# A retention head's output made token by token, normed by ScalarE sums along the row, and turned afterwards

## The chip, the cores and the metric

One NeuronCore of one Trainium2 chip runs the whole program. The metric is device time in microseconds (us) of one execution. The engines are TensorE (PE; its weight loads are shown apart as PEld), VectorE (DVE), ScalarE (ACT), GpSimd (POOL) and SyncE (SP), which issues the weight stream's transfers. They run their own instruction lists and meet only at semaphores.

## The reference, cut to what matters

The program is one block with sparse attention (8 heads of 64) and retention (4 heads, keys 128 wide, values 256 wide) on 512 tokens by 1024 features, a feed-forward part, and then two layers of another block. The change lies in the retention heads:

```
def head_group_norm(o, w):
    mean = jnp.mean(o, axis=-1, keepdims=True)
    var = jnp.mean(jnp.square(o - mean), axis=-1, keepdims=True)
    return (o - mean) * lax.rsqrt(var + EPS) * w.astype(jnp.float32)
...
o = o_inner + jnp.moveaxis(o_cross, 0, 1)
...
o_r = head_group_norm(o_r, ret_gn_w[layer]) * jax.nn.silu(g_ret...)
y_b = o_r.astype(x.dtype).reshape(B, S, RET_V_W) @ w_ret_branch[layer]
```

For each head `o` is (masked, decayed scores) times values: 512 tokens by 256 features. Each token is normed over its 256 features and multiplied by the gate silu(g).

## The kernel before, in words

**Layout.** Activations lie with features on the 128 partitions and the 512 tokens along the row. The weights stream in as units of 128x1024; PE makes one output tile of a unit from 24 matmuls of 128x512 (for each of 8 slices k: `w_hi*a_hi`, `w_hi*a_lo`, `w_lo*a_hi`, L832 to L834), since each operand is split into a rounded high part and the rest. ACT makes `w_hi` (`hi_part`, L434), POOL makes `w_lo` (`lo_part`, L377, four instructions a unit), DVE takes the result out of its bank (L1392).

**The retention stage.** It has 4 heads t = 0 to 3 of 8 slots j = 0 to 7. A slot is one unit on PE, with other work laid between its slices k by `beside`. Beside each retention head runs one attention query head: in slot j PE makes scores (L1028), DVE their maxima (L1586 to L1592), ACT the exponentials with row sums (L548), DVE the probabilities (L1618 to L1624), PE turns these with transposes (L1035, L1036; placed at k = 6, or k = 5 in slots 3 and 7), ACT copies the turned tiles out of the banks (`copy_transposed`, L557, into `pt`), and PE multiplies them by the values (L1047). The order on every engine is written out by hand, so a waiting instruction holds all that stands behind it. After the unit of a slot PE waits for the copied probabilities (`probs_copied`), then makes the scores of the next slot (not in slot 7) and the value products. The next head's first scores follow those of slot 7.

**The head's output before.** In slot 6 (`retention_products(5)`) `ret_values` makes the output with features on partitions: values stationary, decayed scores `rp` moving, for both halves e of the features, into banks `b_r0` and `b_r1` (L1015). ACT copies both out (L613, L614) into `rq` and `rk` (tiles of `h`). DVE adds the two, PE multiplies the sum by a matrix of ones (L1077, slot 7, k = 3), DVE takes the mean off (L1832), squares and adds (L1836 to L1839) into `ssum`, PE sums these with ones (`square_sum`, L867, behind the unit of slot 7), and ACT takes the root (`tile_root`, L458), for which it loads a table and then the exponentials' table again. In the next head DVE inverts the root in four pieces (`inverse_root`, L1733), and POOL multiplies gate by output (`gate_output`, L395) and by the inverse (`scale_output`, L403) between its `lo_part` instructions. ACT and DVE then split the result into `y_hi` (`output_hi`, L570) and `y_lo` (`output_lo`, L1746).

**ACT in slot 7**: the exponentials, `hi_part`, two copies that turn the next query's halves (`turn_query`, L527), a table load and the gate's Silu (L623, tile `rg`), the copy of the turned probabilities (L557), table, root, table.

**The end of the stage**: PE starts the next part, U_YA, whose first two units it does in two pieces (slices k = 0 to 2 of both, then k = 3 of both, which wait for `attention_out_rounded`). Unit 2 of U_YA needs the banks of unit 0, which DVE empties with two multiplications (L1865). DVE copies one element (L1856) to signal `tables_used`, on which ACT's transfer of x into `h` waits.

Of the kernel before, what the change touches and what calls it, by code (L numbers as in the profile page):

```python
# [147 lines left out]
def build(nc, stream, xT, tab, decay, rope, par1, par2, pT, out):  # L148
    ctx = ExitStack()
    with ctx:  # L150
# [68 lines left out]
        head_sum = token_root  # L219
        hid = w1(at + 256, 128).rearrange("p (k c) -> p k c", c=64)  # L220
# [5 lines left out]
        rq, rk = h[:, 4, :], h[:, 5, :]  # L226
        qt, q_turned = tile_d, m[:, 7, :]
# [68 lines left out]
        root_inverted = sem("root_inverted")  # L296
        output_gated = sem("output_gated")
        output_scaled = sem("output_scaled")
# [70 lines left out]
        def _(pool):  # L369
# [17 lines left out]
            def quarters():  # L387
                return [(e, slice(c * S // 2, (c + 1) * S // 2)) for e in range(2) for c in range(2)]

            def gate_output(t):  # L390

                pool.wait_ge(activated, t + 2)
                pool.wait_ge(squares_ready, t + 2)
                for e, cols in quarters():
                    pool.tensor_tensor(rg[:, e, cols], rg[:, e, cols], (rq, rk)[e][:, cols], ALU.mult)\  # L395
                        .then_inc(output_gated, 1)

            def scale_output(t):

                pool.wait_ge(output_gated, 4 * t + 4)  # L400
                pool.wait_ge(root_inverted, t + 1)
                for e, cols in quarters():
                    pool.tensor_tensor(rg[:, e, cols], rg[:, e, cols], ssum[:, cols], ALU.mult)\  # L403
                        .then_inc(output_scaled, 1)
# [18 lines left out]
        def _(act):  # L423
# [142 lines left out]
            def output_hi(t):  # L566

                act.wait_ge(output_scaled, 4 * t + 4)
# [52 lines left out]

# [192 lines left out]
        def _(pe):  # L814
# [181 lines left out]
            for t in range(RH):  # L996
# [14 lines left out]
                def ret_values(e, dst):  # L1011
                    at = 0
                    for a in range(QT):
                        n = S - a * P
                        ins = pe.matmul(dst[:, a * P:S], rv[:, a, e * P:(e + 1) * P], rp[:, at:at + n],  # L1015
                                        start=a == 0, stop=a == QT - 1, skip_group_check=True)
                        at += n
                    ins.then_inc(product_ready, rps.up())
# [32 lines left out]
                def retention_products(j):  # L1051
# [17 lines left out]
                    if j == 5:  # L1069
                        pe.wait_ge(product_read, rfree.due())  # L1070
                        pe.wait_ge(value_rows_copied, 2 * t + 2)
                        ret_values(0, b_r0)
                        ret_values(1, b_r1)
# [1457 lines left out]
```

## Time and profile before

| | |
|---|---|
| time, 3 runs | 2577.57 us median (2577.47 to 2578.15) |
| the profiled execution | 2577.84 us, span 2576.1 us |
| PE busy | 2558.5 us of the span (99%) |
| DVE, ACT, POOL busy | 1486.3, 838.6, 1514.9 us |
| granted TensorE clock over the span | 1.00 |

A matmul's shown duration includes its way through the array, so neighbouring matmuls overlap in the rows; what one costs is the distance from its start to the next one's start. A multiplication of two unrounded fp32 operands is shown as two matmul records, a transpose as one. "Idle before" in brackets is the time an engine stood idle, and behind the arrow what ended it.

### The profile page before, as it was taken

The page shows a single profiled execution, that of the slowest core. Times are in us where ns is not written, and L with a number is a line of the kernel's source. Part 1 is how long each engine was busy: PE and PEld are TensorE (multiplying, and loading weights), DVE is VectorE, ACT ScalarE, POOL GpSimd, SP SyncE. Part 2 cuts the span into 40 slices and gives each one's busy share as a digit, 9 for nine tenths or more (in the row PEclk, how much of TensorE's full clock was granted, in tenths as well). Part 3 has the DMA queues.
Part 4 walks back from the last instruction along what each step waited for, and adds up shares of the span by engine and source line. Part 5 has one row for each costly group of instructions (what it writes and reads, how often), then busy time and mean ns, then how long its engine had stood idle before and what let it go on. Part 6 is the DMA issues. An engine that isn't in the chain of part 4 may idle for free.

```text
span 2576.1 us, 32876 instructions
## 1 busy us (share of the span) xinstructions
PE 2558.5 (99%) x11723; PEld 2062.5 (80%) x11723; DVE 1486.3 (58%) x2084; ACT 838.6 (33%) x1157; POOL 1514.9 (59%) x1820
## 2 busy tenths in 40 slices
PE   8999999999999999999999999999999999999999
PEld 7767778888888887778888888888778888888887
DVE  7756774487474737845583442754773448344275
ACT  5444442233222343354321111134334432111112
POOL 7634446666666755555565655765554556565576
PEclk9999999999999999999999999999999999999999
DMA  5311113222222332222322222233222222222223
GB/s 208 115 66 50 55 61 131 98 83 98 99 97 98 109 111 82 83 82 82 106 99 98 98 97 92 89 114 105 77 85 84 82 106 98 99 98 97 92 89 130
DMA packets 36829, 247.44 MB, mean 96 GB/s; under 512 B 4464, under 2 KB 4848, under 8 KB 7792
## 3 DMA queue, kind: packets, MB, share of 16 engines
q1 hardware_dynamic: 34704, 238.57, 26.2%
q10 hardware_dynamic: 2016, 7.35, 0.8%
q8 instruction: 76, 1.25, 0.2%
q14 instruction: 33, 0.27, 0.0%
HBM read 243.81 MB, written 2.10 MB: 95 GB/s over the span
## 4 chain that ended last, share of the span: by engine, by line
PE 31%; POOL 30%; issue 22%; DVE 0%; POOLq 0%; DMA 0%; ACT 0%; DVEq 0%; SPq 0%; ACTq 0%
POOL w_lo L377 30%; PE bank L832 7%; PE bank L834 7%; PE bank L833 7%; PE both L833 3%; PE both L834 3%; PE both L832 3%; PE bank L1281 0%; PE both L1257 0%; PE bank L1243 0%; PE bank L1241 0%; PE bank L1242 0%; DMA raw<-stream 0%; POOLq L415 0%; POOLq L374 0%
## 5 line engine op out<-in xcount | busy, mean ns | idle before, releaser
L377 POOL TENSOR_TENSOR w_lo<-raw,w_hi 128x256 fp32r<-128x256 f32 x1784 | 1492.6, 868 | 964.2 <-ACT w_hi L434 963.2
L434 ACT ACTIVATE w_hi<-raw 128x1024 fp32r<-128x1024 f32 x446 | 469.1, 1056 | 981.6 <-PE bank L834 476.8
L832 PE MATMUL bank<-a_hi,w_hi 128*128 128x512 f32 x1440 | 582.1, 404 | 0.0
L834 PE MATMUL bank<-a_hi,w_lo 128*128 128x512 f32 x1440 | 562.3, 390 | 0.0
L833 PE MATMUL bank<-a_lo,w_hi 128*128 128x512 f32 x1440 | 561.3, 390 | 0.0
L832 PEld LDWEIGHTS bank<-a_hi,w_hi 128*128 128x128 f32 x1440 | 270.5, 188 | 63.7 <-issue 10.3
L834 PEld LDWEIGHTS bank<-a_hi,w_lo 128*128 128x128 f32 x1440 | 270.3, 188 | 58.3
L833 PEld LDWEIGHTS bank<-a_lo,w_hi 128*128 128x128 f32 x1440 | 270.9, 188 | 54.7 <-issue 3.1
L832 PE MATMUL bank<-y_hi,w_hi 128*128 128x512 f32 x696 | 272.4, 391 | 0.0
L834 PE MATMUL bank<-y_hi,w_lo 128*128 128x512 f32 x696 | 270.9, 389 | 0.0
L833 PE MATMUL bank<-y_lo,w_hi 128*128 128x512 f32 x696 | 270.8, 389 | 0.0
L832 PE MATMUL both<-a_hi,w_hi 128*128 128x512 f32 x560 | 219.1, 391 | 0.0
L834 PE MATMUL both<-a_hi,w_lo 128*128 128x512 f32 x560 | 217.9, 389 | 0.0
L833 PE MATMUL both<-a_lo,w_hi 128*128 128x512 f32 x560 | 217.9, 389 | 0.0
L832 PE MATMUL both<-y_hi,w_hi 128*128 128x512 f32 x504 | 196.5, 390 | 0.5 <-DVE y_lo L1398 0.2
L834 PE MATMUL both<-y_hi,w_lo 128*128 128x512 f32 x504 | 196.1, 389 | 0.0
L833 PE MATMUL both<-y_lo,w_hi 128*128 128x512 f32 x504 | 196.1, 389 | 0.0
L832 PEld LDWEIGHTS bank<-y_hi,w_hi 128*128 128x128 f32 x696 | 130.7, 188 | 27.3 <-issue 0.5
L834 PEld LDWEIGHTS bank<-y_hi,w_lo 128*128 128x128 f32 x696 | 130.6, 188 | 27.3
L833 PEld LDWEIGHTS bank<-y_lo,w_hi 128*128 128x128 f32 x696 | 130.7, 188 | 27.2 <-issue 0.5
L548 ACT ACTIVATE prob<-both,small 128x128 f32<-128x128 f32 (+3 forms) x128 | 66.3, 523 | 203.0 <-DVE small L1592 202.8
L1890 DVE TENSOR_TENSOR h<-bank,h 128x512 f32<-128x512 f32 x56 | 38.7, 691 | 154.5 <-PE bank L834 153.8
(343 smaller groups left out, 3279.6 us busy)
## 6 DMA issues: line engine op xcount, KB each, us to landing
raw<-stream SPq DMA_DIRECT2D x223, 1024.0 KB, 4.8
h<-xT SPq DMA_DIRECT2D x8, 256.0 KB, 5.9
h<-xT ACTq DMA_DIRECT2D x1, 2048.0 KB, 8.1
outT<-h SPq DMA_DIRECT2D x8, 256.0 KB, 2.3
h<-decay ACTq DMA_DIRECT2D x1, 1024.0 KB, 4.8
h<-rope ACTq DMA_DIRECT2D x1, 1024.0 KB, 9.3
prob<-pT ACTq DMA_DIRECT2D x2, 512.0 KB, 4.4
par<-par ACTq DMA_DIRECT2D x2, 408.0 KB, 3.3
```

The costliest lines, as they stand in the source:

```text
L377: pool.tensor_tensor(w_lo[:, s, part], raw[:, s, part], w_hi[:, s, part], ALU.subtract).then_inc(lo_done, 1)
L434: act.activation(w_hi[:, s, cols], raw[:, s, cols], ACT.Copy).then_inc(hi_done, 1)
L548: ins = act.activation(dst, src, ACT.Exp, bias=small[:, b:b + 1], scale=last_scale, accum_out=small[:, b + 4:b + 5])
L832: pe.matmul(dst, w_hi[:, s, cols], rhs_hi(k), start=start and k == 0, stop=False)
L833: pe.matmul(dst, w_hi[:, s, cols], rhs_lo(k), start=False, stop=False)
L834: ins = pe.matmul(dst, w_lo[:, s, cols], rhs_hi(k), start=False, stop=stop and k == nk - 1)
L1890: leave(u0, j, V.tensor_tensor(h[:, n, :], bank4(j), h[:, n, :], ALU.add))
```

## The change

- `ret_values(i)` now makes the output with tokens on partitions: for token tile i (four of 128) the pieces of `rp` are stationary and the values, 256 columns, move: 10 matmuls instead of 8, the same number of columns in all. Tiles 0 and 1 lie in `b_r0`, 2 and 3 in `b_r1`.
- ACT copies the four tiles of 128x256 out with a row sum each (`accum_out`), where it made two copies of 128x512.
- In slot 7 DVE scales the four sums to means (`output_mean`); ACT, ahead of the gate's Silu, squares the four tiles with the mean as bias, again with a row sum; it takes the root of a 128x4 tile instead of a 128x512 one.
- Both multiplications by ones on PE (L1077 and the `square_sum` of the stage) are gone, and DVE's sum, mean, squares and the four-piece inversion.
- In slot 0 of the next head DVE inverts 128x4 numbers and scales the four tiles by mean and root (`output_norm`). In slot 1, k = 3, PE turns the tiles with eight transposes back into `b_r0`, `b_r1` (`turn_outputs`), and DVE multiplies them by the gate (`output_gate`).
- POOL does none of this any more.
- For the last head `turn_outputs` stands on PE between the two pieces of U_YA's units 0, 1 and unit 2, and `output_gate` on DVE ahead of the `tables_used` copy and of U_YA's multiplications.

```diff
@@ gpsimd
-                    if j == 7 and t > 0:
-                        scale_output(t - 1)
-                    if j == 10:
-                        gate_output(t)
                     lo_part(t * RET_UNITS + U_RET + j, j % 4)
-            scale_output(RH - 1)
@@ scalar, slots 6 and 7
                     if j == 6:
                         rps.up(2)
                         act.wait_ge(product_ready, rps.now())
-                        act.activation(rq, b_r0[:, :], ACT.Copy).then_inc(outputs_copied, 1)
-                        act.activation(rk, b_r1[:, :], ACT.Copy).then_inc(outputs_copied, 1)
-                        rps.up(1)
+                        for i, rows in enumerate(out_rows):
+                            ins = act.activation(rows, (b_r0, b_r1)[i // 2][:, i % 2 * RDV:(i % 2 + 1) * RDV],
+                                                 ACT.Copy, accum_out=out_mean[:, i:i + 1])
+                        ins.then_inc(outputs_copied, 1)
                     if j == 7:
-
+                        act.wait_ge(output_mean_ready, t + 1)
+                        for i, rows in enumerate(out_rows):
+                            ins = act.activation((ssum[:, :], tile_c)[i // 2][:, i % 2 * RDV:(i % 2 + 1) * RDV], rows, ACT.Square,
+                                                 bias=out_mean[:, i:i + 1], accum_out=out_root[:, i:i + 1])
+                        ins.then_inc(output_squares_done, 1)
                         act.wait_ge(evac, u0 + 11)
                         act.activation(rg, rg, ACT.Silu).then_inc(activated, res.up())
                     copy_transposed([(pt[:, :, 0:n], scores[:, :, 0:n])])
                     if j == 7:
-                        tile_root(ssum[:, :], b_r1[:, :], 1.0 / RDV)
+                        load_table(ACT.Sqrt)
+                        act.wait_ge(output_squares_done, t + 1)
+                        act.activation(out_root, out_root, ACT.Sqrt, bias=eps, scale=1.0 / RDV)\
+                            .then_inc(root_ready, root.up())
                         load_table(ACT.Exp if t < RH - 1 else ACT.Sigmoid)
@@ tensor
+                def ret_values(i):
+                    dst = (b_r0, b_r1)[i // 2][:, i % 2 * RDV:(i % 2 + 1) * RDV]
+                    for a in range(i + 1):
+                        at = sum(S - c * P for c in range(a)) + (i - a) * P
+                        ins = pe.matmul(dst, rp[:, at:at + P], rv[:, a, :], start=a == 0, stop=a == i,
+                                        skip_group_check=True)
+                    if i % 2 == 1:
+                        ins.then_inc(product_ready, rps.up())
+
+                def turn_outputs(t):
+
+                    pe.wait_ge(output_normed, t + 1)
+                    for e in range(2):
+                        for i in range(QT):
+                            ins = pe.transpose((b_r0, b_r1)[e][:, i * P:(i + 1) * P],
+                                               out_rows[i][:, e * P:(e + 1) * P], ident)
+                    ins.then_inc(output_turned, 1)
@@
-                    if j == 6:
-                        pe.wait_ge(outputs_copied, 2 * t + 2)
-                        pe.wait_ge(retention_input_ready, rin.due())
-                        pe.matmul(b_r0[:, :], ones, tile_c, start=True, stop=True)\
-                            .then_inc(product_ready, rps.up())
@@
+                    if k == 3 and j == 1 and t > 0:
+                        turn_outputs(t - 1)
@@
-                    if j == 7:
-                        square_sum()
@@ behind the two pieces of U_YA's units 0 and 1
+            turn_outputs(RH - 1)
@@ vector
+            def output_norm(t):
+
+                V.wait_ge(root_ready, root.due())
+                V.reciprocal(out_root, out_root).then_inc(vector_step, steps.up())
+                V.wait_ge(vector_step, steps.now())
+                for i, rows in enumerate(out_rows):
+                    ins = V.tensor_scalar(rows, rows, out_mean[:, i:i + 1], out_root[:, i:i + 1],
+                                          ALU.add, ALU.mult)
+                ins.then_inc(output_normed, 1)
+
+            def output_gate(t):
+
+                V.wait_ge(activated, res.due())
+                V.wait_ge(output_turned, t + 1)
+                for e in range(2):
+                    V.tensor_tensor(rg[:, e, :], (b_r0, b_r1)[e][:, :], rg[:, e, :], ALU.mult)\
+                        .then_inc(output_gated, 1)
@@
                 if last is not None and j == 0:
                     attention_out(last, 1)
+                    output_norm(last)
+                if last is not None and j == 1:
+                    output_gate(last)
@@ behind the stage
             attention_out(RH - 1, 1)
+            output_norm(RH - 1)
             attention_rounded(RH - 1, 1)
-            for quarter in range(4):
-                inverse_root(RH - 1, quarter)
-            V.wait_ge(output_gated, 4 * RH)
+            output_gate(RH - 1)
+            V.wait_ge(output_gated, 2 * RH)
             V.tensor_copy(small[:, 20:21], rq[:, 0:1]).then_inc(tables_used, 1)
```

Where the instructions stand is shown at three places, first before and then changed. The first is ACT's list in slot 7 of a head (the second one), from `hi_part` to the first table load behind the copy of the turned probabilities.

```order
L434 ACTIVATE w_hi<-raw 128x1024 [waits unit_done,block_landed_1]
L527 ACTIVATE m<-m 64x512 x2
L623 ACT_TABLE_LOAD
L623 ACTIVATE rg<-rg 128x1024 [waits unit_evacuated]
L557 ACTIVATE pt<-both 128x1024 [waits probs_transposed,values_added]
L450 ACT_TABLE_LOAD
```

```order
L415 ACTIVATE w_hi<-raw 128x1024 [waits unit_done,block_landed_1]
L508 ACTIVATE m<-m 64x512 x2
L605 ACTIVATE ssum,small<-h,small 128x256 [waits output_mean_ready]
L605 ACTIVATE ssum,small<-h,small 128x256
L605 ACTIVATE tile_c,small<-h,small 128x256 x2
L609 ACT_TABLE_LOAD
L609 ACTIVATE rg<-rg 128x1024 [waits unit_evacuated]
L538 ACTIVATE pt<-both 128x1024 [waits probs_transposed,values_added]
L431 ACT_TABLE_LOAD
```

Four squares (L605), the first of which waits for `output_mean_ready`, now stand between `turn_query` (L508) and the table load of the Silu, and so ahead of the copy into `pt` (L538, before L557). The second place is DVE's list from the last probabilities of slot 0 of the second head through slot 1 up to the maxima of slot 2.

```order
L1709 TENSOR_TENSOR cmp_prob<-bank,ta 64x512 [waits lower_half_copied,probs_ready]
L1586 TENSOR_TENSOR both<-both,cst 128x2x128 [waits scores_ready,attention_out_read]
L1589 TENSOR_REDUCE small<-both 128x2 [waits vector_step]
L1592 TENSOR_SCALAR small<-small 128x2 [waits vector_step]
L1392 TENSOR_TENSOR ta<-bank,rstd 128x512 [waits unit_done,vector_step,max_ready]
L1439 STREAM_SHUFFLE tb<-ta 128x512 [waits unit_evacuated]
L1618 RECIPROCAL small<-small 128x2 [waits exp_ready]
L1621 TENSOR_SCALAR prob<-prob,small 128x256 [waits vector_step]
L1624 TENSOR_SCALAR prob<-prob,small 128x256 [waits vector_step]
L1447 TENSOR_TENSOR tb<-tb,h 128x512 [waits vector_step,probs_ready]
L1448 TENSOR_TENSOR ta<-ta,h 128x512
L1586 TENSOR_TENSOR both<-both,cst 128x2x128 [waits scores_ready]
```

```order
L1703 TENSOR_TENSOR cmp_prob<-bank,ta 64x512 [waits lower_half_copied,probs_ready]
L1725 RECIPROCAL small<-small 128x4 [waits root_ready,attention_out_read]
L1728 TENSOR_SCALAR h<-h,small 128x256 [waits vector_step]
L1728 TENSOR_SCALAR h<-h,small 128x256 x3
L1580 TENSOR_TENSOR both<-both,cst 128x2x128 [waits scores_ready]
...
L1615 TENSOR_SCALAR prob<-prob,small 128x256 [waits vector_step]
L1618 TENSOR_SCALAR prob<-prob,small 128x256 [waits vector_step]
L1737 TENSOR_TENSOR rg<-bank,rg 128x512 [waits output_turned,activated,probs_ready]
L1737 TENSOR_TENSOR rg<-bank,rg 128x512
L1441 TENSOR_TENSOR tb<-tb,h 128x512 [waits vector_step]
L1442 TENSOR_TENSOR ta<-ta,h 128x512
L1580 TENSOR_TENSOR both<-both,cst 128x2x128 [waits scores_ready]
```

The inversion and four scalings (L1725, L1728) came in between `attention_out` (L1703) and the maxima of slot 1 (L1580), and two multiplications (L1737) between the probabilities of slot 1 and the two products L1441, L1442. The third place is the end of the stage on DVE, from `attention_out` of the last head to the multiplications that empty the banks of U_YA's unit 0.

```order
L1709 TENSOR_TENSOR cmp_prob<-bank,ta 64x512 [waits lower_half_copied]
L1718 TENSOR_TENSOR cmp_prob<-cmp_prob,vn 64x512 [waits cmp_out_copied,attention_out_read]
L1722 CAST y_hi<-cmp_prob 64x512 [waits vector_step]
L1724 TENSOR_TENSOR y_lo<-cmp_prob,y_hi 64x512 [waits vector_step]
L1733 RECIPROCAL ssum<-ssum 128x128 [waits root_ready,attention_out_rounded]
L1733 RECIPROCAL ssum<-ssum 128x128 x3
L1856 COPY small<-h 128x1 [waits output_gated,root_inverted,vector_step]
L1865 TENSOR_TENSOR m<-both,m 128x512 [waits vector_step,unit_done,activated,to_activate]
L1865 TENSOR_TENSOR m<-both,m 128x512
```

```order
L1703 TENSOR_TENSOR cmp_prob<-bank,ta 64x512 [waits lower_half_copied]
L1725 RECIPROCAL small<-small 128x4 [waits root_ready,attention_out_read]
L1728 TENSOR_SCALAR h<-h,small 128x256 [waits vector_step]
L1728 TENSOR_SCALAR h<-h,small 128x256 x3
L1712 TENSOR_TENSOR cmp_prob<-cmp_prob,vn 64x512 [waits cmp_out_copied]
L1716 CAST y_hi<-cmp_prob 64x512 [waits vector_step]
L1718 TENSOR_TENSOR y_lo<-cmp_prob,y_hi 64x512 [waits vector_step]
L1737 TENSOR_TENSOR rg<-bank,rg 128x512 [waits output_turned,activated,attention_out_rounded]
L1737 TENSOR_TENSOR rg<-bank,rg 128x512
L1842 COPY small<-h 128x1 [waits output_gated]
L1851 TENSOR_TENSOR m<-both,m 128x512 [waits vector_step,unit_done,activated,to_activate]
L1851 TENSOR_TENSOR m<-both,m 128x512
```

The first of the two L1737 waits for `output_turned`, which PE gives behind both pieces of U_YA's units 0 and 1, and all that stands behind it, L1851 (before L1865) included, comes after it.

## Rows read from the trace of the kernel before

**Rows 1.** The page: busy time by engine, share of the span, instructions.

```profile
PE 2558.5 (99%) x11723; PEld 2062.5 (80%) x11723; DVE 1486.3 (58%) x2084; ACT 838.6 (33%) x1157; POOL 1514.9 (59%) x1820
```

**Rows 2.** Timeline of PE, third head, slots 6 and 7.

```profile
291.74 4.47 PE L1015 MATMUL bank<-work 128*128 128x512 f32 x16
...
306.57 0.27 PE L1035 MATMUL both<-cst,prob 128*128 128x128 f32 x1
...
307.34 0.27 PE L1036 MATMUL both<-cst,prob 128*128 128x128 f32 x1
...
309.30 0.40 PE L834 MATMUL bank<-a_hi,w_lo 128*128 128x512 f32 x1
309.85 1.13 PE L867 MATMUL bank<-ssum,cst 128*128 128x512 f32 x2 [0.15 <-DVE ssum L1839]
310.90 1.09 PE L1047 MATMUL bank<-pt,work 128*64 128x128 f32 x16
```

**Rows 3.** Timeline of PE's weight loads, slot 7, first head.

```profile
164.72 0.85 PEld L1047 LDWEIGHTS bank<-pt,work 128*64 128x64 f32 x16 [0.81 <-ACT pt L557]
```

**Rows 4.** Timeline of ACT, third head, slots 6 and 7; last row first head.

```profile
299.07 0.81 ACT L557 ACTIVATE pt<-both 128x768 f32<-128x768 f32 x1 [0.51 <-PE both L1036]
...
305.89 1.28 ACT L527 ACTIVATE m<-m 64x512 f32<-64x512 f32 x2
307.19 1.28 ACT L623 ACT_TABLE_LOAD   x1
308.48 1.06 ACT L623 ACTIVATE rg<-rg 128x1024 f32<-128x1024 f32 x1
309.45 1.00 ACT L557 ACTIVATE pt<-both 128x1024 f32<-128x1024 f32 x1
...
163.66 1.00 ACT L557 ACTIVATE pt<-both 128x1024 f32<-128x1024 f32 x1
```

**Rows 5.** Timeline of ACT, two exponentials of 256 columns with a row sum.

```profile
320.49 0.47 ACT L548 ACTIVATE prob<-both,small 128x256 f32<-128x256 f32 x1 [3.05 <-DVE small L1592]
...
320.95 0.47 ACT L548 ACTIVATE prob<-both,small 128x256 f32<-128x256 f32 x1
```

**Rows 6.** Timelines, slot 7: DVE third head, DVE fourth head, PE fourth head.

```profile
305.80 0.55 DVE L1624 TENSOR_SCALAR prob<-prob,small 128x512 f32<-128x512 f32 x1
...
377.01 0.55 DVE L1624 TENSOR_SCALAR prob<-prob,small 128x512 f32<-128x512 f32 x1
...
382.12 1.09 PE L1047 MATMUL bank<-pt,work 128*64 128x128 f32 x16
```

**Rows 7.** Timeline of DVE, third head, slots 1 and 2; last row POOL.

```profile
247.88 0.43 DVE L1586 TENSOR_TENSOR both<-both,cst 128x256 f32<-128x256 f32 x1 [2.37 <-PE both L1028]
...
250.96 0.41 DVE L1621 TENSOR_SCALAR prob<-prob,small 128x256 f32<-128x256 f32 x1
251.41 0.80 DVE L1624 TENSOR_SCALAR prob<-prob,small 128x256 f32<-128x256 f32 x1
...
255.21 0.43 DVE L1586 TENSOR_TENSOR both<-both,cst 128x256 f32<-128x256 f32 x1 [0.71 <-PE both L1028]
...
251.32 3.76 POOL L377 TENSOR_TENSOR w_lo<-raw,w_hi 128x256 fp32r<-128x256 f32 x4 [3.11 <-ACT w_hi L434]
```

**Rows 8.** Timelines of DVE, then PE, at U_YA's unit 2.

```profile
393.12 1.29 DVE L1865 TENSOR_TENSOR m<-both,m 128x512 f32<-128x512 f32 x2 [1.24 <-PE both L834]
...
394.55 0.47 PE L832 MATMUL both<-y_hi,w_hi 128*128 128x512 f32 x1 [0.21 <-DVE m L1865]
```

**Rows 9.** Timeline of PE at the program's start.

```profile
8.17 0.77 PE L902 MATMUL both<-a_hi,w_hi 128*128 128x512 f32 x1 [8.17 <-DVE a_lo L1473]
...
11.30 0.63 PE L903 MATMUL both<-a_lo,w_hi 128*128 128x512 f32 x1
11.72 0.62 PE L902 MATMUL both<-a_hi,w_hi 128*128 128x512 f32 x1
...
12.41 0.39 PE L902 MATMUL both<-a_hi,w_hi 128*128 128x512 f32 x1
```

More of the change, by code:

```diff
@@ L219, in build @@
         head_sum = token_root
+        out_mean = small[:, 16:20]
+        out_root = small[:, 0:16].rearrange("p (i c) -> p i c", c=4)[:, :, 2]
         hid = w1(at + 256, 128).rearrange("p (k c) -> p k c", c=64)
@@ L226, in build @@
         rq, rk = h[:, 4, :], h[:, 5, :]
+        out_rows = [(rq, rk)[i // 2][:, i % 2 * RDV:(i % 2 + 1) * RDV] for i in range(QT)]
         qt, q_turned = tile_d, m[:, 7, :]
@@ L295, in build @@
         gelu_ready = sem("gelu_ready")
-        root_inverted = sem("root_inverted")
         output_gated = sem("output_gated")
-        output_scaled = sem("output_scaled")
+        output_mean_ready = sem("output_mean_ready")
+        output_squares_done = sem("output_squares_done")
+        output_normed = sem("output_normed")
+        output_turned = sem("output_turned")
         output_rounded = sem("output_rounded")
@@ L1009, in ret_transposes @@
                     ins.then_inc(product_ready, rps.up())
[L1011 to L1018, printed above, removed]
+                def ret_values(i):
[13 more added lines that the diff above has]
+                    ins.then_inc(output_turned, 1)
                 def attention_scores(j):
@@ L1071, in retention_products @@
                         pe.wait_ge(value_rows_copied, 2 * t + 2)
-                        ret_values(0, b_r0)
-                        ret_values(1, b_r1)
-                    if j == 6:
-                        pe.wait_ge(outputs_copied, 2 * t + 2)
-                        pe.wait_ge(retention_input_ready, rin.due())
-                        pe.matmul(b_r0[:, :], ones, tile_c, start=True, stop=True)\
-                            .then_inc(product_ready, rps.up())
+                        for i in range(QT):
+                            ret_values(i)
                 def compressed_branch(j):
@@ L1726, in attention_rounded @@
                 V.wait_ge(attention_out_rounded, rounded.now())
-            def inverse_root(t, quarter):
-                if quarter == 0:
-                    V.wait_ge(root_ready, root.due())
-                cols = slice(quarter * P, (quarter + 1) * P)
-                ins = V.reciprocal(ssum[:, cols], ssum[:, cols])
-                if quarter < 3:
-                    ins.then_inc(vector_step, steps.up())
-                else:
-                    V.wait_ge(vector_step, steps.now())
-                    ins.then_inc(root_inverted, 1)
-                    V.wait_ge(root_inverted, t + 1)
-                    res.due()
+            def output_norm(t):
[12 more added lines that the diff above has]
+                        .then_inc(output_gated, 1)
             def output_lo(t):
@@ L1749, in output_lo, with output_mean @@
                 V.wait_ge(y_tile_ready, y_rdy.now())
-            def outputs_in(t):
-                V.wait_ge(outputs_copied, 2 * t + 2)
+            def output_mean(t):
+                V.wait_ge(outputs_copied, t + 1)
                 rps.due(2)
-                V.tensor_tensor(tile_c, rq, rk, ALU.add).then_inc(retention_input_ready, rin.up())
-                V.wait_ge(retention_input_ready, rin.now())
+                V.tensor_scalar(out_mean, out_mean, -1.0 / RDV, None, ALU.mult).then_inc(output_mean_ready, 1)
             def slot(t, j):
@@ L1764, in slot @@
                     if last is not None:
-                        V.wait_ge(output_gated, 4 * last + 4)
+                        V.wait_ge(output_gated, 2 * last + 2)
                     rope_sum(rq).then_inc(vector_step, steps.up())
@@ L1811, in slot @@
                     compressed_product()
-                if last is not None and j in (3, 4):
-                    inverse_root(last, 2 * j - 6)
-                    inverse_root(last, 2 * j - 5)
                 if j == 5:
@@ L1827, in slot @@
                 if j == 7:
-                    V.wait_ge(product_ready, rps.due())
+                    output_mean(t)
                     V.tensor_copy(small[:, 24:26], par[:, C1_GN + 2 * t:C1_GN + 2 * t + 2])\
                         .then_inc(vector_step, steps.up())
-                    for o in (rq, rk):
-                        V.scalar_tensor_tensor(out=o, in0=b_r0[:, :], scalar=-1.0 / RDV, in1=o,
-                                               op0=ALU.mult, op1=ALU.add)\
-                            .then_inc(vector_step, steps.up())
                     V.wait_ge(vector_step, steps.now())
-                    V.tensor_tensor(tile_a, rq, rq, ALU.mult).then_inc(vector_step, steps.up())
-                    V.tensor_tensor(ssum[:, :], rk, rk, ALU.mult).then_inc(vector_step, steps.up())
-                    V.wait_ge(vector_step, steps.now())
-                    V.tensor_tensor(ssum[:, :], ssum[:, :], tile_a, ALU.add)\
-                        .then_inc(squares_ready, sums.up())
-                    V.wait_ge(squares_ready, sums.now())
                     if t < RH - 1:
```

17 lines of the change are left out of this document (1 added, 16 removed).

## The prediction, made before the changed kernel was run

> **What bounds the kernel now.** I read the page first: PE is busy for 99% of the span, every other engine for 59% or less [rows 1]. So a change counts only by what it takes from PE's instruction list, puts into it, or makes PE wait for. Then the timeline of PE through the stage. In slot 7 of the third head the unit's last matmul starts at 309.30, the multiplication by ones (`square_sum`, L867) at 309.85 after 0.15 us of idle, and the value products (L1047) at 310.90 [rows 2]. The reader is to see that PE hardly waits, and that L867 fills the time in which ACT still works on what L1047 reads: ACT's copy into `pt` begins at 309.45 and lasts 1.00, to 310.45, which is 0.45 before L1047 starts [rows 4]. In the first head there is no such room: the copy ends at 163.66 + 1.00 = 164.66, and L1047's weight load starts at 164.72, released by it [rows 3, 4]. DVE is as close: it finishes the probabilities at 305.80 + 0.55 = 306.35, and the transposes that read them start at 306.57, their weight load before them [rows 2, 6]. So slot 7 is where PE, ACT and DVE meet, and the change works on all three there.
>
> **PE's own work.** `ret_values` moves the same columns: 8 matmuls with 2,560 columns before, 10 of 256 after. Before, the 16 records run 4.4 us [rows 2]; between records of 128 and of 512 columns no pause shows in that sum, so I take 0 for it, 0.4 as the upper end for all heads together. Eight transposes come in: from 306.57 to 307.34 there are seven steps of 0.11, so eight cost 0.88 us a head, 3.5 us for four. The `square_sum` goes: 310.90 less 309.85 is 1.05, and with the idle before it up to 1.3. L1077, a matmul of the same shape, goes too, about 0.9. If nothing waited, PE would gain 4 x (1.3 + 0.9) and lose 3.5.
>
> **What takes the place of L1077.** It stands at k = 3 of slot 7, ahead of the transposes. Without it PE is at the transposes 0.9 earlier, but the probabilities are ready at 306.35 as before, since DVE's and ACT's work for them starts from the scores of slot 6. PE was there about when they were; now it waits. Worth: nothing.
>
> **What takes the place of `square_sum`.** ACT gets four squares between `turn_query` and the Silu's table load, ahead of the `pt` copy. No row before has a square with bias and row sum; the nearest is the exponential of 256 columns with both, a start every 320.95 - 320.49 = 0.46 us [rows 5]. It reads from a bank, the square from SBUF. The upper end is the 64x512 copy from SBUF, 1.28 for two, 0.64 each [rows 4]; the lower 0.40. I take 0.46, the same form, and 0.15 for the last sum's own end: 2.0 us. The Trainium skill (ScalarE: Activation LUTs, What ACT_TABLE_LOAD costs) gives 280 ns + 0.833 ns a column for an instruction with a pointer as bias, less 93 ns of overlap; by that page it would be 0.40 each without the sum's reading, 1.6 in all.
> Behind the squares stand the table load (1.28), the Silu (0.97 from start to start) and the copy (1.00), all unchanged [rows 4]. In the third head: squares start at 307.19, when DVE's mean is there (306.35 + about 0.2). The copy ends at 310.45 + 2.0 = 312.45, L1047 starts at 312.5 in place of 310.90: +1.6. The second head's slot 7 has the same order, +1.6. In the first head L1047 already hung on the copy: +2.0. In the fourth there is no `turn_query`, so ACT waits for the mean: 377.01 + 0.55 + 0.2 [rows 6]. POOL is no longer held at `gate_output` then, so its `lo_part` starts beside DVE's last probabilities and can stretch them as in [rows 7]: I add 0.4. That is 378.2, + 2.0 + 1.28 + 0.97 + 1.0 = 383.4, against L1047 at 382.12 [rows 6]: +1.3. Sum of the four: 6.5 us. PE thus stands about 2.9 us idle behind the unit of slot 7 (309.53 to 312.5), where it stood 0.15. ACT's table, root, table follow the copy as before; the root of 128x4 is shorter, so the next head's first exponentials move with PE and cost nothing more.
>
> **Slot 6.** The four copies with sums are at most 4 x 0.46 in place of 2 x 0.5, so up to 0.85 later for ACT; it stood idle 0.51 ahead of its next copy into `pt` [rows 4]. Cost 0, upper end 0.3 a head in three heads.
>
> **DVE in the next head's slots 0 and 1.** The four scalings of 256 columns come ahead of the maxima of slot 1, the two gate multiplications (0.65 each, as L1865 with a bank as source [rows 8]) ahead of slot 2's. DVE's idle there is 2.37 and 0.71 [rows 7], and PE comes 0.88 later in slot 1: 3.96 in all. A scaling of 256 columns took 0.41 alone and 0.80 beside POOL [rows 7]. Alone: 4 x 0.45 + 0.2 + 1.35 = 3.35, no stall. Beside POOL: 4 x 0.84 + 0.2 + 1.35 = 4.9, about 1 us late. POOL's `lo_part` runs in slot 0 at just that place, and DVE has little idle time until slot 3, so I take 0.5 us a head for three heads, 1.5 us; ends 0 and 1.2 a head. The Trainium skill (SBUF — State Buffer, Who interferes with whom) holds that a VectorE scaling in its two-port mode and a GpSimd instruction exclude each other for a whole instruction; by that rule each scaling could wait a whole POOL instruction, and this term would go to its upper end. The 0.80 against 0.41 agrees.
> DVE no longer does the sum, squares and inversion (3.4 us behind the last head); no row shows PE waiting for them but the 0.15 above, so that is worth nothing more.
>
> **The end of the stage.** `turn_outputs` of the last head stands behind both pieces of U_YA's units 0 and 1, and DVE's `output_gate` waits for it ahead of the multiplications that empty unit 0's banks. Before, DVE did these from 393.12 while PE worked on unit 1, and PE's unit 2 waited 0.21 [rows 8]. Now, from the end of the transposes: 1.3 for the two gate multiplications, 0.2 for the one-element copy, 1.29 for L1865, and about 0.2 of hand-over: PE is idle 3.0, so +2.8. Queued behind on ACT: the transfer of x, which waits for `tables_used`, and two weight units; they are needed slots later.
>
> **The sum**, against the profiled execution of 2577.84 us: slot 7 +6.5, transposes +3.5, lateness of DVE +1.5, end of the stage +2.8, together +14.3: 2592.1. The median is 0.27 below that execution, so 2591.8 us.
>
> **Rivals.**
> *PE's lighter list decides (faster).* If ACT's copy were done when PE has finished its unit, PE would gain 4 x 2.2 - 3.5 = 5.3: 2572.3. For it the copy must end at 309.6 in the third head; it ends at 310.45 without any square, so even free squares leave L1047 no earlier than 310.5. Against it as well: the probabilities at 306.35. Chance 0.04.
> *It cancels (within 0.2%).* With squares that cost hardly anything, no lateness of DVE: slot 7 comes to -1, transposes 3.5, end 2.8: +5, about 2582.8. The exponentials' 0.46 speaks against it. Chance 0.07.
> *The clock falls.* PE now stands idle some 3 us four or five times. At the start, after 8.17 us of idle, its 512-column matmuls began 0.42 apart and showed 0.63, later 0.39 [rows 9]: the lower of 1.2 and 2.4 GHz, though the granted clock reads 1.00. If each wait brings some 4 us at that rate, each costs 2 us more: +8 to +10, 2601. No row shows an idle stretch of 3 us inside the program, so none excludes it. The Trainium skill (TensorE: Matmul & The Clock Gate, Part 1) says that idleness throttles the clock back, and that busy time releases it. The start agrees. Chance 0.10.
> *DVE is the new bound in slots 0 to 3.* If the gate multiplications are stretched too, each of three heads is 2 us late at slot 3: 2591.8 + 4.5 = 2596.3. Chance 0.14.
> *The forecast*: 0.65, with its own range 2587 to 2596.
>
> **How the numbers follow.** A measurement of this kernel can tell about 0.2%, 5.2 us, from no change. Low end: squares 0.40 (-1.0), no lateness (-1.5), no stretching (-0.4), end of stage 0.5 less: +10.9, 2588; I go to 2586.5, half-way to the case that cancels. High end: squares 0.64 (+2.9), lateness 1.2 a head (+2.1), slot 6 (+0.9), `ret_values` (+0.4): 2598.1; with a part of the clock's case 2599.5. Faster 0.04, same 0.07, slower 0.89.
>
> **What would show it.** L1047 of slot 7 released by ACT's copy, with PE idle about 2.9 us before it in three heads; the transposes of slot 7 released by DVE's probabilities after 0.8 of idle; squares 0.46 apart; about 3 us idle ahead of U_YA's unit 2, released by DVE's L1851; PE's busy time down by some 5 us while the span grows. It would be wrong if the squares take under 0.2 each, if ACT's idle time hides them, or if DVE's maxima of slots 1 to 3 slip by more than 1 us.

## The result and the profile after

| | before | after |
|---|---|---|
| time, median | 2577.86 us (2577.47 to 2578.66, 4 runs) | 2599.39 us (2599.12 to 2600.13, 4 runs) |
| ratio | | 1.0084, 95% interval 1.0072 to 1.0097 |
| span of the profiled execution | 2576.1 us | 2597.3 us |
| granted TensorE clock, mean | 1.000 | 0.996 |

The change costs 21.5 us. The page of the changed kernel gives for the engines:

```profile
PE 2563.6 (99%) x11755; PEld 2074.9 (80%) x11755; DVE 1471.4 (57%) x2076; ACT 847.3 (33%) x1213; POOL 1495.5 (58%) x1788
```

PE's busy time rose by 5.1 us against [rows 1], though the added transposes (3.5 us) are less than the multiplications by ones that went (some 7 us). So something made the same matmuls longer. The view of what PE waited for (engine, line, what it waited for: us in total, times, longest) names the new waits:

```profile
PE bank L1045 <- ACT pt L538: 12.4, 4, 3.5
...
PE both L821 <- DVE m L1851: 3.1, 1, 3.1
PE both L1033 <- DVE prob L1618: 2.7, 5, 0.7
```

Of the five waits for L1618 two, in the first head's early slots, stood before too (0.61 and 0.69 then, 0.32 and 0.69 now); three of 0.55 are new. Slot 7 of the second head, on ACT and then on PE (timelines; the value products, L1047 before, are L1045 now, the transposes L1033, the query scores L1026):

```profile
239.12 1.28 ACT L508 ACTIVATE m<-m 64x512 f32<-64x512 f32 x2
240.42 0.51 ACT L605 ACTIVATE ssum<-h,small 128x256 f32<-128x256 f32 x1
...
241.92 0.49 ACT L605 ACTIVATE tile_c<-h,small 128x256 f32<-128x256 f32 x1
...
242.52 1.28 ACT L609 ACT_TABLE_LOAD   x1
243.81 1.06 ACT L609 ACTIVATE rg<-rg 128x1024 f32<-128x1024 f32 x1
244.78 1.00 ACT L538 ACTIVATE pt<-both 128x1024 f32<-128x1024 f32 x1
```

```profile
239.63 0.33 PE L1033 MATMUL both<-cst,prob 128*128 128x128 f32 x1 [0.55 <-DVE prob L1618]
...
242.41 0.40 PE L823 MATMUL bank<-a_hi,w_lo 128*128 128x512 f32 x1
245.83 1.14 PE L1045 MATMUL bank<-pt,work 128*64 128x128 f32 x16 [3.02 <-ACT pt L538]
246.90 0.58 PE L1026 MATMUL both<-work,td 64*128 64x128 f32 x1
...
248.65 0.63 PE L823 MATMUL bank<-a_hi,w_lo 128*128 128x512 f32 x1
249.08 0.63 PE L821 MATMUL bank<-a_hi,w_hi 128*128 128x512 f32 x1
```

The four squares take from 240.42 to 242.52, and table load, Silu and copy follow without a gap; the copy ends at 245.78 and PE, idle since 242.81, starts at 245.83. This is the third head's picture of [rows 2, 4] with the copy 2.1 us later. Ahead of it PE waits 0.55 for DVE's probabilities, in the place of L1077. New is what stands behind the wait: the unit's matmuls start 0.43 us apart and show 0.63, as at the program's start [rows 9]. Granted clock by stretch of the changed kernel (columns: stretch, length, busy time and count of PE, PEld, DVE, ACT, POOL, granted clock, DMA share, GB/s), each from the end of a long wait, and one stretch behind slot 3 of the second head for comparison:

```profile
166.70:174.00 7.30, 7.27 (x39) 5.82 (x40) 4.84 (x12) 5.40 (x11) 1.76 (x3) 0.77 0.01 2
205.70:213.00 7.30, 7.30 (x49) 6.03 (x48) 6.72 (x13) 3.33 (x8) 3.56 (x4) 1.00 0.00 0
245.80:254.00 8.20, 8.17 (x44) 6.53 (x45) 5.68 (x13) 5.85 (x12) 2.59 (x4) 0.79 0.01 2
321.10:329.00 7.90, 7.90 (x43) 6.27 (x44) 5.25 (x12) 5.73 (x12) 2.16 (x3) 0.78 0.01 2
396.10:404.00 7.90, 7.86 (x39) 6.30 (x40) 3.87 (x9) 7.83 (x9) 0.00 (x0) 0.78 0.01 2
413.80:421.00 7.20, 7.13 (x24) 5.76 (x25) 1.24 (x2) 0.07 (x1) 2.80 (x4) 0.76 0.90 349
```

All five stretches behind waits of 2.8 to 3.5 us have 0.76 to 0.79, which is part of the time at 1.2 GHz and part at 2.4; the other has 1.00.

The last head's output, on PE and DVE, with the rows that answer to [rows 8]:

```profile
409.76 1.03 PE L1014 MATMUL bank<-cst,h 128*128 128x128 f32 x8
413.87 0.64 PE L821 MATMUL both<-y_hi,w_hi 128*128 128x512 f32 x1 [3.07 <-DVE m L1851]
414.31 0.63 PE L822 MATMUL both<-y_lo,w_hi 128*128 128x512 f32 x1
...
410.93 1.29 DVE L1737 TENSOR_TENSOR rg<-bank,rg 128x512 f32<-128x512 f32 x2 [6.75 <-PE bank L1014]
412.25 0.15 DVE L1842 COPY small<-h 128x1 f32<-128x1 f32 x1
412.43 1.29 DVE L1851 TENSOR_TENSOR m<-both,m 128x512 f32<-128x512 f32 x2
```

The eight transposes (L1014) run first, then DVE's two gate multiplications (L1737, L1842 is the one-element copy), then what empties the banks (L1851); PE stands idle 3.07 where it stood 0.21, and goes on at half rate.

**Where the 21 us are.** From one head's value products of slot 7 to the next one's the rows give 74.97, 71.21 and 71.22 us before and 79.10, 75.27 and 75.04 after. The first head's are 2.01 later, the way from the fourth's to U_YA's unit 2 is 17.73 in place of 12.43, and the 24 matmuls of that unit take 7.14 in place of 5.56. Together 2.01 + 4.13 + 4.06 + 3.82 + 5.30 + 1.58 = 20.9 of the span's 21.2. What of it is the clock follows from the starts of the same instructions before and after, from the value products to where the matmuls are 0.23 apart again: 1.55, 1.50, 1.51 and 1.55 us longer than before, and 1.58 in the last unit. A head's eight transposes take 0.79 to the next matmul's start, and that matmul's own step is 0.08 longer, 0.87 together; the last head's cost 0.88. What is left of each way between heads is slot 7's. So:

| | forecast | measured |
|---|---|---|
| slot 7, four heads | 6.5 | 2.0 + 1.7 + 1.7 + 1.4 = 6.8 |
| transposes | 3.5 | 3 x 0.87 + 0.88 = 3.5 |
| DVE late in slots 0 to 3 | 1.5 | 0 |
| end of the stage | 2.8 | 3.07 - 0.21 = 2.9 |
| half-rate matmuls | 0 | 7.7 |
| sum | 14.3 | 20.9 |

### The profile page after: what moved, and what is told of

It is laid out like the page before. It is cut to its first block, busy times and chain, and to the rows that moved or that the text cites. A ratio compares the mean times of both kernels' runs of the same rounds, so it can differ in the third digit from the quotient of the medians.

```text
span 2597.3 us, 32939 instructions
## 1 busy us (share of the span) xinstructions
PE 2563.6 (99%) x11755; PEld 2074.9 (80%) x11755; DVE 1471.4 (57%) x2076; ACT 847.3 (33%) x1213; POOL 1495.5 (58%) x1788
## 4 chain that ended last, share of the span: by engine, by line
PE 40%; POOL 32%; issue 23%; ACT 2%; DVE 1%; DMA 1%; POOLq 0%; SPq 0%; DVEq 0%; ACTq 0%
POOL w_lo L382 32%; PE bank L821 9%; PE bank L823 8%; PE bank L822 8%; PE both L821 3%; PE both L823 3%; PE both L822 3%; DMA raw<-stream 1%; PE both L1026 1%; PE bank L1004 1%; PE bank L1045 1%; PE bank L1275 0%; PE both L1251 0%; ACT w_hi L415 0%; PE bank L1237 0%
```

## The experiments

All ratios are to the kernel before, measured beside each experiment on the same chip (2577.80 and 2577.74 us there, 2577.86 above, so that a difference to the changed kernel carries about 0.1 us of doubt from this). Three theories were to be told apart: that PE's idle stretches cost time twice, as waits and by the clock behind them (A); that the slow matmuls come from something else in the new order, and idleness is not their cause (B); and that the late engine is not ACT's squares but something that only moves when they are moved (C).

**Squares in slot 6.** The mean goes to DVE's slot 6 and the squares behind slot 6's copy on ACT, where ACT stood idle 3.6 us; the lines taken out stood in slot 7, ahead of the Silu.

```diff
-                        act.wait_ge(output_mean_ready, t + 1)
-                        for i, rows in enumerate(out_rows):
-                            ins = act.activation(..., rows, ACT.Square, ...)
...
                     copy_transposed([(pt[:, :, 0:n], scores[:, :, 0:n])])
+                    if j == 6:
+                        act.wait_ge(output_mean_ready, t + 1)
+                        for i, rows in enumerate(out_rows):
+                            ins = act.activation(..., rows, ACT.Square, ...)
...
@@ vector
                 if j == 6:
+                    output_mean(t)
...
                 if j == 7:
-                    output_mean(t)
```

> The changed kernel with the mean on DVE and the four squares on ACT moved from slot 7 to slot 6, behind that slot's copy of the turned probabilities. Theory A (ACT's squares make PE wait about 3 us in slot 7 of each head, and the wait lets TensorE's clock fall, so that the next matmuls run at half rate): the waits shrink from 3.0 to 3.5 us to about 1 to 1.5, the matmuls behind them stay about 0.23 us apart, and the time falls by 4 x 2.1 + 6.3 = 14.7 us, to about 2585. Theory B (the slow matmuls behind the wait come from something else in the new order, not from the idle time): only the squares' time comes back, 8.4 us, 2591, and the slow matmuls stay. Theory C (moving the squares makes slot 6 or slot 7's exponentials late instead): less than 8 us.

Measured: 2583.47 us (2581.41 to 2584.7), ratio 1.0021 (1.0011 to 1.0030), 15.9 us less than the changed kernel. PE's waits for ACT's copy and for U_YA's banks, and the granted clock behind the first and second head's slot 7 and behind U_YA's wait:

```profile
PE bank L1046 <- ACT pt L538: 3.3, 3, 1.4
PE both L822 <- DVE m L1852: 3.1, 1, 3.1
```

```profile
164.80:172.00 7.20, 7.17 (x46) 5.75 (x46) 4.75 (x12) 5.78 (x12) 1.66 (x3) 1.00 0.01 2
240.20:248.00 7.80, 7.74 (x50) 6.05 (x50) 5.31 (x12) 5.80 (x13) 2.22 (x4) 1.00 0.01 2
...
398.70:406.00 7.30, 7.25 (x25) 5.88 (x26) 1.23 (x2) 0.06 (x1) 2.80 (x4) 0.78 0.91 352
```

Waits of 1.4 and 0.9 us are left, the clock behind them is 1.00, and only U_YA's wait of 3.07 is still followed by 0.78. This is A's case, and C is out. Since the edit also moves work, it does not by itself exclude B; the run that fills the wait does.

**The end of the stage redone**, in the changed kernel. `silu_done` is the Silu's count, taken where `output_gate` stood.

```diff
-            turn_outputs(RH - 1)
             for j in range(2, YA_UNITS):
                 unit(U_YA, j, 2, [bank4(2 * j), bank4(2 * j + 1)], y_op(8), 4)
+                if j == 2:
+                    turn_outputs(RH - 1)
@@ vector
-            output_gate(RH - 1)
-            V.wait_ge(output_gated, 2 * RH)
-            V.tensor_copy(small[:, 20:21], rq[:, 0:1]).then_inc(tables_used, 1)
...
                 leave(U_YA, j, ins)
+                if j == 2:
+                    output_gate(RH - 1, silu_done)
+                    V.wait_ge(output_gated, 2 * RH)
+                    V.tensor_copy(small[:, 20:21], rq[:, 0:1]).then_inc(tables_used, 1)
```

> The changed kernel with only the end of the stage redone: the last head's eight transposes stand behind U_YA's unit 2 on PE, DVE's gate multiplications and the tables_used copy behind the emptying of unit 2's banks. Theory A: the idle 3.07 us ahead of unit 2 goes and with it 1.7 us of half-rate matmuls behind it, so about 4.7 us less, 2594.7. Theory B (slow matmuls not from idle time): 3 us less, 2596.4. Theory C: the gate's wait only moves to a later unit, and nothing is gained.

Measured: 2595.35 us (2595.06 to 2595.53), ratio 1.0067 (1.0050 to 1.0083): 4.0 us less than the changed kernel, against 4.7 expected by A and 3 by B. PE's wait there, from the same view as above:

```profile
PE both L821 <- DVE m L1850: 0.2, 1, 0.2
```

The four waits of slot 7 are all there still. The time alone lies between A and B, but the trace decides: the granted clock behind the second head's slot 7 and in U_YA's unit 2 (stretches as above):

```profile
245.70:253.70 8.00, 7.94 (x36) 6.34 (x37) 4.62 (x11) 5.52 (x12) 1.54 (x3) 0.60 0.01 2
411.50:419.00 7.50, 7.43 (x37) 6.26 (x38) 2.81 (x5) 0.00 (x0) 2.56 (x4) 1.00 0.21 87
```

With the wait gone U_YA runs at the full rate, as A has it: 2.9 of waiting and 1.6 of half rate are saved. In this execution the lower level lasted longer behind the second head's wait of 3.02, 2.9 us lost in place of 1.5, and what follows unit 2 took 0.5 less: 2.9 + 1.6 - 1.4 + 0.5 = 3.6, the difference of the two spans (2597.3 and 2593.7).

**PE's wait filled with work.** The sharpest test of A: the changed kernel, with three multiplications into a bank that nobody reads behind the unit of slot 7.

```diff
+                    if j == 7:
+                        pe.wait_ge(outputs_copied, t + 1)
+                        for _ in range(3):
+                            pe.matmul(b_r0[:, :], ones, cst[:, 0:S], start=True, stop=True)
                     pe.wait_ge(probs_copied, ptr.due())
```

> The changed kernel with work added to PE: behind the unit of slot 7 of each head, three multiplications of 128x512 constants by ones into a bank that nobody reads (2.6 us of PE work a head), where PE otherwise stands idle. Theory A: the added work lies in the wait, the clock stays at its upper level, the next matmuls are 0.23 us apart, and the kernel gets faster by about 6.3 us although it does more: 2593. Theory B (the cause is not PE's idleness): no change or up to 1 us slower, and the matmuls behind L1045 stay 0.43 apart.

Measured: 2592.14 us (2590.82 to 2593.33), ratio 1.0054 (1.0038 to 1.0071): 7.3 us faster than the changed kernel, with 12 multiplications of 0.86 (10 us) more work on PE. PE's wait for ACT's copy, and the granted clock behind the second head's slot 7 and behind U_YA's wait, which was left as it is:

```profile
PE bank L1045 <- ACT pt L538: 2.1, 4, 0.9
```

```profile
244.00:252.00 8.00, 7.96 (x50) 6.05 (x50) 5.53 (x13) 5.79 (x12) 2.44 (x4) 1.00 0.01 2
...
407.40:415.00 7.60, 7.52 (x26) 6.11 (x27) 1.35 (x3) 0.22 (x2) 2.83 (x4) 0.78 0.90 349
```

Nothing else was touched: the value products still start when ACT's copy ends, and ACT's list is the same. The ways from one head's value products to the next one's and on to U_YA are 1.58, 1.52, 1.51 and 1.57 us shorter, which are the half-rate terms of the table within 0.03; 0.6 of the rest lies in what follows U_YA's unit 2, and is not explained. So it is PE's standing idle, and not the order of the work, that makes the matmuls behind it slow. B is out.

**ACT's weight alone, on the kernel before.** Four squares of constants ahead of the Silu of slot 7; both multiplications by ones stay.

```diff
                     if j == 7:
+                        for i in range(4):
+                            act.activation(y_lo[:, 6 + i // 2, i % 2 * 256:(i % 2 + 1) * 256], cst[:, 0:256],
+                                           ACT.Square, bias=eps, accum_out=small[:, 16 + i:17 + i])
                         act.wait_ge(evac, u0 + 11)
```

> The kernel before, with nothing of the change but its weight on ACT: four squares of 128x256 constants with a row sum ahead of the gate's Silu in slot 7, into a tile that is free. It still has both multiplications by ones. Theory A: ACT's copy ends 2.0 us later, L1047 starts 1.6 us later in three heads and 2.0 in the first, 6.8 us in all, 2584.6; PE's idle time ahead of it is only about 1.7 us, since square_sum still stands there, and no half-rate matmuls follow. If a wait of 1.7 us is enough for the clock to fall: about 13 us, 2591. If the squares don't hold up PE: no change.

Measured: 2584.97 us (2584.34 to 2587.21), ratio 1.0030 (1.0019 to 1.0040), +7.2. PE's value products of slot 7 in the first two heads, and the clock behind them:

```profile
166.44 1.09 PE L1049 MATMUL bank<-pt,work 128*64 128x128 f32 x16 [2.08 <-ACT pt L557]
...
244.66 1.09 PE L1049 MATMUL bank<-pt,work 128*64 128x128 f32 x16 [1.63 <-ACT pt L557]
```

```profile
166.40:174.00 7.60, 7.56 (x41) 6.06 (x42) 3.82 (x8) 5.79 (x11) 6.34 (x10) 0.78 0.01 2
244.60:252.00 7.40, 7.34 (x46) 5.75 (x46) 3.85 (x8) 6.19 (x13) 6.19 (x10) 1.00 0.01 2
```

Two things came out. The squares alone hold PE up by 1.7 us in three heads; in the fourth, where no `turn_query` stands ahead of them, by little (idle 0.17), since these squares wait for no mean. And an idle stretch of 2.08 brought the clock down, one of 1.63 did not. The value products of the first head start 1.7 later than before, the way from them to the second head's is 3.25 longer, to the third head's 1.7, to the fourth's 0.2. With 1.55 of half rate inside the 3.25 that is 1.7 + 1.7 + 1.7 + 0.2 of waiting, 6.9 of the 7.2 in all, but not as I had split it: I had expected no fall at all, and the fourth head's 1.6. The eight times fall in two groups, five of 2584.3 to 2585.2 us and three of 2587.0 to 2587.2. The profile is of one of the five; whether one more fall makes the others is not shown.

**A third of the filling.** As above, with one multiplication instead of three. One execution only.

> The changed kernel with one multiplication of constants by ones (0.86 us of PE work) instead of three behind the unit of slot 7. PE's idle time there should be 2.6 us in the first head and about 2.1, 2.1 and 1.9 in the others. In the earlier runs idle stretches of 2.8 us and more, and one of 2.08, were followed by matmuls at half rate, stretches of 1.63 and less were not. Theory A: the first head's is followed by half-rate matmuls, the others are near the bound and can go either way; time between 2593 and 2599. Theory B (idleness is not the cause): half-rate matmuls as in the changed kernel in all four.

Measured: 2599.45 us, as slow as the changed kernel. Granted clock behind the waits of 2.65, 2.16, 2.16 and 1.96 us (first to fourth head) and of 3.07 (U_YA):

```profile
166.40:174.00 7.60, 7.60 (x41) 6.03 (x42) 4.79 (x12) 5.48 (x11) 1.71 (x3) 0.78 0.01 2
245.40:253.00 7.60, 7.54 (x41) 6.15 (x42) 4.22 (x11) 5.53 (x12) 1.13 (x2) 0.78 0.01 2
320.70:329.00 8.30, 8.25 (x36) 6.55 (x37) 4.92 (x12) 5.51 (x11) 1.84 (x3) 0.60 0.01 2
397.30:405.00 7.70, 7.65 (x45) 6.36 (x46) 3.66 (x9) 7.62 (x9) 0.00 (x0) 1.00 0.00 0
413.50:421.00 7.50, 7.50 (x21) 5.95 (x22) 1.18 (x2) 0.01 (x1) 2.80 (x4) 0.60 0.91 342
```

The shortest wait is followed by no fall, the other four are, two of them with 0.60 in place of 0.78: there the lower level lasted longer (3.1 and 2.9 us lost in place of 1.5 and 1.6), which made up for the head that was spared. Here a third of the filling was worth nothing, the whole of it 7.3 us.

**Both moved.** Squares in slot 6 and the end of the stage redone (the edits of the first two experiments together).

> The changed kernel with both edits of the first runs: mean and squares in slot 6, and the last head's transposes and gate behind U_YA's unit 2. Theory A adds them up: 2583.5 less 3.1 of idle and 1.6 of half-rate matmuls at the end of the stage, 2578.8, which this measurement cannot tell from the kernel before. No half-rate matmuls inside the program at all. If the two overlap: 2580 to 2583.

Measured: 2578.82 us (2578.52 to 2579.43), ratio 1.0004 (0.9995 to 1.0013). No wait above 1.41 us is left inside the program, and no half-rate matmul in the stage either. So the two edits give back 20.6 of the 21.5 us; the tokens-first output as such costs nothing that this measurement can tell, and gains nothing.

**The copy ahead of the Silu**, on top of that, to take away the waits of 0.9 to 1.4 us that are left in slot 7.

```diff
+                        copy_transposed([(pt[:, :, 0:n], scores[:, :, 0:n])])
                         act.wait_ge(evac, u0 + 11)
                         act.activation(rg, rg, ACT.Silu).then_inc(activated, res.up())
-                    copy_transposed([(pt[:, :, 0:n], scores[:, :, 0:n])])
+                    if j < 7:
+                        copy_transposed([(pt[:, :, 0:n], scores[:, :, 0:n])])
```

> e5 with ACT's copy of the turned probabilities in slot 7 ahead of the Silu and its table load. Theory A: PE's idle time of 0.92 to 1.41 us ahead of the value products goes (3.5 us over four heads). But ACT still has three table loads behind it before the next head's exponentials, about 6.1 us with Silu and root, so these come about 1.4 us later than PE's scores allow, against a room of about 0.5 before the transposes of slot 0: up to 0.9 us of new idle time in three heads. Together 1 to 3.5 us less than e5: 2575.3 to 2578. Rival: the Silu's tables don't matter, and all 3.5 us come back.

Measured: 2578.58 us (2578.34 to 2579.35), ratio 1.0003 (0.9994 to 1.0012): nothing gained, a miss. The waits for ACT's copy are gone from slot 7, but PE waits anew for the probabilities of slot 0 of the third head (timeline), and in total (waits):

```profile
244.75 0.33 PE L1036 MATMUL both<-cst,prob 128*128 128x128 f32 x1 [0.66 <-DVE prob L1622]
```

```profile
PE both L1036 <- DVE prob L1622: 4.7, 8, 0.7
```

Of the eight, two are the old ones of the first head, three are slot 7's 0.55 and three are new, in slot 0. ACT's three table loads between the copy and the next head's exponentials decide there: the last ends at 242.76 and the exponentials start at 242.88, while PE was 1.6 us earlier at the value products than without the edit (238.28 against 239.84). The mechanism was the expected one, up to 0.9 us in each of three heads, and it took 0.75 + 0.66 + 0.67 = 2.1. Against it stand the 1.41 + 0.92 + 0.92 = 3.2 of the waits taken away. That leaves 1.1, of which the time shows 0.2. The starts of the same instructions in both traces say where the rest went. The first head keeps 0.5 of what its slot 7 gives. In the third head PE is 0.59 ahead of the run before up to slot 7, 1.59 ahead at the value products, 0.71 behind slot 0's transposes and 0.58 behind slot 1's, so that two slots take back the whole 1.0. In the fourth head 0.44 of the 0.59 is lost in U_YA, at the matmul that waits for DVE's `attention_rounded` in the next run.

**And the transposes of slot 7 one slice later** (`k == (5 if j == 3 else 6)`).

> e6 with the transposes of slot 7 at k = 6 instead of k = 5, so that PE has 0.7 us more work before it needs DVE's probabilities, for which it now idles 0.56. If only slot 7 decided, 4 x 0.56 = 2.2 us less than e6. If ACT's chain of table loads to the next head's first exponentials is what decides (theory A), the gain is given back in slot 0 of three heads, and 0.6 us is left.

Measured: 2579.16 us (2578.5 to 2579.5), ratio 1.0005 (0.9996 to 1.0014). The 0.55 us waits of slot 7 are gone, and those of slot 0 grew from 0.7 to 1.36:

```profile
PE both L1036 <- DVE prob L1622: 5.1, 5, 1.4
PE both L824 <- DVE y_lo L1722: 0.8, 1, 0.8
```

What slot 7 gives, slot 0 takes; the fourth head's 0.6 was lost again to a new wait of 0.80 for DVE's `attention_rounded` at the end of the stage. No version beats the kernel before.

## Why the prediction was right or wrong

**The step that failed** is a term that the sum left at nothing. It had PE idle for some 3 us four or five times, but took the matmuls behind each wait at 2.4 GHz, and left half-rate matmuls to the rival "The clock falls", at "Chance 0.10". They ran at 1.2 GHz for a while behind every one of the five waits: 7.7 us, 1.5 to 1.6 each, where the rival had 2 each and 8 to 10 in all. With it the time came out 7.6 us above the predicted one, outside the forecast's own 2587 to 2596 and above the 2598.1 that its terms could reach; that it still lies below 2599.5 is owed to the part of the clock's case that I had added there, not to the forecast. The sign of PE's busy time was wrong for the same reason: I had named it as down by some 5 us, and it rose by 5.1. The page of the Trainium skill cited beside it (TensorE: Matmul & The Clock Gate, Part 1) was on the right side, with a granted clock of 0.76 to 0.79 behind the five waits; I let the absence of a row with a 3 us idle stretch count as evidence for the upper level, which it was not.

**What takes the place of `square_sum`**: right in mechanism and nearly in size, 6.8 against 6.5. The squares take 0.50 from start to start with 2.1 in all, where I had 0.46 and 2.0. Moving them, and adding only them to the kernel before, showed it.

**What takes the place of L1077**: right. PE waits 0.55 for the probabilities in three heads.

**PE's own work**: right. Eight transposes cost 0.87; `ret_values` as tokens takes 4.55 to the start of the second matmul behind it, where it took 4.56, so the two extra matmuls cost nothing.

**Slot 6**: right, no wait of PE there.

**DVE in slots 0 and 1**: mis-sized. I put 1.5 us, it was 0. The rows of DVE in the third head, slots 0 and 1:

```profile
251.76 2.77 DVE L1728 TENSOR_SCALAR h<-h,small 128x256 f32<-128x256 f32 x4
255.47 0.43 DVE L1580 TENSOR_TENSOR both<-both,cst 128x256 f32<-128x256 f32 x1 [0.94 <-PE both L1026]
...
259.84 1.29 DVE L1737 TENSOR_TENSOR rg<-bank,rg 128x512 f32<-128x512 f32 x2
```

Beside POOL a scaling took 0.69, four of them 2.77, not the 3.4 of the slower row in [rows 7], and DVE was ready 0.94 us before the scores of slot 1 came. In the last head, without POOL, the four took 1.38. The end that I called "no stall" was the true one. By the rule of the Trainium skill (SBUF — State Buffer, Who interferes with whom) this term would have gone to its upper end; that there is stretching agrees with it, 0.69 against 0.35 alone, but each scaling lost 0.34, where POOL's instructions beside it took 0.74 each, so none waited for a whole one, and the idle time covered the rest.

**The end of the stage**: right, idle 3.07 and +2.9, shown by the run that redid it.

**The faster rival** failed on the point it named: in the first three heads the copy was not ready by the end of the unit, not even with the squares elsewhere, when it came 0.9 to 1.4 us late.

**The low end of the range** was reckoned wrong: 2577.57 + 10.9 is 2588.5, and half-way from there to 2582.8 is 2585.7, not 2586.5. Nothing hung on it.

## What to carry to other kernels

Work that is taken off the bounding engine gains nothing where it was filling that engine's wait for another's chain: count back from the wait, not from the instruction removed. Where a sum leaves a busy TensorE idle for some microseconds, add half-rate matmuls behind the wait, here mostly 1.5 to 1.6 us after each of 2.8 to 3.5 and twice 2.9, and look for a version whose single waits are short; the same work put one slot earlier on ACT gave back 15.9 us. And where an engine's chain runs across a slot boundary, as ACT's three table loads do, a gain ahead of it shows up as a wait behind it.

## What the runs showed of the hardware that was not expected

- In the changed kernel the granted clock reads 1.00 through all five idle stretches and falls where work goes on, now at once and now a little later. In the four heads it reads 1.00, 0.93, 0.87 and 0.92 over the value products behind the wait and 0.61, 0.50, 0.50 and 0.50 over the 2 us after them; in U_YA it reads 0.57 over the first 0.9 us, and with one multiplication as filling 0.52 over the first 0.9 us of the second head's value products.
- Idle stretches of TensorE inside the stage and what followed, over all profiled executions: up to 1.4, 1.63 (twice) and 1.96 us no fall; 2.08, 2.16 (twice), 2.65 and all of 2.8 to 3.5 a fall. Between 1.63 and 2.65 each length stands on one or two waits of one execution. Behind one of the 2.16, one of the 3.07 (both in the run with one multiplication) and one of the 3.02 (the end of the stage redone) the granted clock of the stretch was 0.60 where it is 0.76 to 0.79 elsewhere, and 2.9 to 3.1 us were lost in place of 1.5 to 1.6. Nothing varied here tells why.
- Ten microseconds of useless matmuls made the kernel 7.3 us faster.
